# Cross-attention of two layers: the second pair of heads is worked before the sample in every attention step

## The reference, cut to what matters

```
def cross_attend(xn, k, v, wq, wo):
    bsz, L, _ = xn.shape
    q = (xn @ wq).reshape(bsz, L, X_HEADS, X_DH)
    s = jnp.einsum('blhd,bmhd->bhlm', q, k).astype(jnp.float32) * (X_DH ** -0.5)
    p = jax.nn.softmax(s, axis=-1).astype(v.dtype)
    o = jnp.einsum('bhlm,bmhd->blhd', p, v).reshape(bsz, L, D_MODEL)
    return o @ wo
```

## Time and profile before

| | |
|---|---|
| median of 3 runs | 2462.33 us (2460.72 to 2467.35) |
| the profiled execution's own time | 2461.94 us |
| its span in the trace | 2460.2 us |
| TensorE busy | 2294.2 us (93%) |
| VectorE, ScalarE, GpSimd busy | 1215.8, 339.8 and 1220.9 us |
| chain that ended last, TensorE's part | 79% |
| TensorE's mean granted clock | 0.948 of full |

### The profile page before, as it was taken

One profiled execution on the slowest core, in us unless ns is written; L12 is line 12 of the kernel. 1 busy time (PEld: TensorE's weight loads), 2 busy tenths in 40 slices (PEclk: granted clock), 3 DMA queues, 4 the chain that ended last, 5 costly groups with the idle time before them and its releaser, 6 DMA issues.

```text
span 2460.2 us, 39360 instructions
## 1 busy us (share of the span) xinstructions
PE 2294.2 (93%) x16133; PEld 2123.2 (86%) x16133; DVE 1215.8 (49%) x2104; ACT 339.8 (14%) x578; POOL 1220.9 (50%) x1185
## 2 busy tenths in 40 slices
PE   7968768999999999999999989999989999999997
PEld 7967667997999999999999965687569799999996
DVE  6675576432535263674756425441543327253363
ACT  4211301212200000120110131110212210000001
POOL 5535676642665566666656500022025256655562
PEclk8988889999999999999999977889889999999998
DMA  5212323310222222233333321332131012222221
GB/s 189 85 69 86 103 99 121 138 69 35 70 86 86 86 76 78 85 118 141 130 144 148 113 104 52 131 131 86 56 137 69 35 69 73 83 86 86 84 71 54
DMA packets 36594, 231.27 MB, mean 94 GB/s; under 512 B 4332, under 2 KB 7404, under 8 KB 10864
## 3 DMA queue, kind: packets, MB, share of 16 engines
q1 hardware_dynamic: 21600, 154.15, 17.8%
q10 hardware_dynamic: 14864, 75.21, 7.8%
HBM read 195.50 MB, written 33.85 MB: 93 GB/s over the span
## 4 chain that ended last, share of the span: by engine, by line
PE 79%; DVE 16%; issue 2%; ACT 2%; DMA 0%; ACTq 0%; DVEq 0%
PE psum L513 60%; PE psum L543 14%; PE psum L529 2%; DVE hl L1899 1%; DVE xnl L1425 1%; DVE hh L1895 1%; DVE xc L1964 1%; PE psum L539 1%; DVE tm L1625 1%; DVE ss L1410 0%; DVE hr L1888 0%; DVE hs L1891 0%; DVE bbq L1649 0%; DVE tm L2178 0%; DVE tm L2177 0%
## 5 line engine op out<-in xcount | busy, mean ns | idle before, releaser
L463 POOL TENSOR_SCALAR whi<-raw 128x512 fp32r<-128x512 f32 x584 | 422.7, 724 | 1150.1 <-PE psum L513 1107.2
L465 POOL TENSOR_TENSOR wlo<-raw,whi 128x512 fp32r<-128x512 f32 x584 | 803.0, 1375 | 48.7
L513 PE MATMUL psum<-xnh,whi 128*128 128x288 f32 (+1 forms) x2816 | 625.5, 300 | 64.2 <-DVE xnl L1425 17.8
L513 PE MATMUL psum<-xnl,whi 128*128 128x288 f32 (+1 forms) x2816 | 618.7, 298 | 0.0
L513 PE MATMUL psum<-xnh,wlo 128*128 128x288 f32 (+1 forms) x2816 | 618.2, 298 | 0.0
L513 PEld LDWEIGHTS psum<-xnh,whi 128*128 128x128 f32 x2816 | 465.5, 192 | 74.2 <-issue 52.2
L513 PEld LDWEIGHTS psum<-xnl,whi 128*128 128x128 f32 x2816 | 464.9, 192 | 0.0
L513 PEld LDWEIGHTS psum<-xnh,wlo 128*128 128x128 f32 x2816 | 464.4, 191 | 0.0
L513 PE MATMUL psum<-hh,whi 128*128 128x288 f32 x1024 | 220.2, 296 | 1.6 <-DVE hl L1899 1.6
L513 PE MATMUL psum<-hl,whi 128*128 128x288 f32 x1024 | 219.3, 295 | 0.0
L513 PE MATMUL psum<-hh,wlo 128*128 128x288 f32 x1024 | 219.3, 295 | 0.0
(11 more groups left out here) (395 smaller groups left out, 2735.0 us busy)
## 6 DMA issues: line engine op xcount, KB each, us to landing
raw<-in_w SPq DMA_DIRECT2D x146, 1024.0 KB, 4.7
C<-in_C ACTq DMA_DIRECT2D x4, 1024.0 KB, 4.8
o_cp<-mvt ACTq DMA_DIRECT2D x4, 1024.0 KB, 3.9
o_cs<-C ACTq DMA_DIRECT2D x4, 1024.0 KB, 3.9
t_xc<-xc ACTq DMA_DIRECT2D x3, 1152.0 KB, 6.5
t_z<-mv ACTq DMA_DIRECT2D x3, 1152.0 KB, 4.1
t_q<-mq ACTq DMA_DIRECT2D x3, 1152.0 KB, 4.1
t_k<-mk ACTq DMA_DIRECT2D x3, 1152.0 KB, 4.2
```

The source lines that it names most:

```text
L463: pool.tensor_scalar(whi[:, s, c], raw[:, s, c], 1.0, 1.0, ALU.mult, ALU.mult).then_inc(S("slab_hi"), 1)
L465: ins = pool.tensor_tensor(wlo[:, s, c], raw[:, s, c], whi[:, s, c].bitcast(F32), ALU.subtract)
L513: ins = pe.matmul(bank(g, 2 * m + b)[:, 0:t1 - t0], W[wi][:, kk, m0 + m, :], r[:, kk, t0:t1], start=(at_first and wi == 0 and r is rh), st ...
```

## The change

The order of the parts becomes first pair, second pair, sample (0, 1, 2) in every step, on every engine and in the order of groups. Nothing is added or removed. The wait of the first output projection asks for all three parts from its first tile on.

```diff
-ATT_ORDER = (0, 2, 1)
+ATT_ORDER = (0, 1, 2)
...
-        for x in ("pT", 0), ("score", 2), ("score", 1), ("pv", 0), ("pT", 2), ("pT", 1), ("pv", 2), ("pv", 1):
+        for x in ("pT", 0), ("score", 1), ("score", 2), ("pv", 0), ("pT", 1), ("pT", 2), ("pv", 1), ("pv", 2):
             g("att", l, *x)
...
                 transposed(l, 0)
+                scores(l, 1)
                 g = GR["att", l, "score", 2]
...
-                scores(l, 1)
                 values(l, 0)
+                transposed(l, 1)
                 transposed(l, 2)
-                transposed(l, 1)
+                values(l, 1)
                 values(l, 2)
-                values(l, 1)
                 for i in range(4):
                     project(GR["xo", l, i], SL["xo", l, i], xnh, xnl,
-                            wait=None if i else lambda kk: pe.wait_ge(S("att_o"), 3 * l + (2 if kk < 4 else 3)))
+                            wait=None if i else lambda kk: pe.wait_ge(S("att_o"), 3 * l + 3))
...
                 exps(0)
                 copy_pT(0)
+                exps(1)
                 exps(2)
-                exps(1)
                 high_o(0)
+                copy_pT(1)
                 copy_pT(2)
-                copy_pT(1)
+                high_o(1)
                 high_o(2)
-                high_o(1)
...
+                row_max(1)
                 row_max(2)
-                row_max(1)
+                prob(1)
                 prob(2)
-                prob(1)
                 low_o(0)
+                low_o(1)
                 low_o(2)
-                low_o(1)
```

## The result

The changed kernel took 2478.09 us (median of 18 runs, 2471.85 to 2481.13) against 2466.55 us of the kernel before (median of 18 runs). The ratio is 1.0043, with a 95% interval of 1.0035 to 1.0052: 0.43% slower, 10.6 us (the two medians by themselves lie 11.5 us apart). The time lies in the range, and the slowdown on the forecast side of the 0.3%. The profiled execution took 2477.77 us, with a span of 2476.0 us.

What follows compares the result with a forecast made beforehand. TensorE, with 79% of the chain, was taken to bound the kernel. Stalls of +3.9 us and low clock of +7.0 us gave +10.9 us on the profiled 2461.94, or 2472.8, given as 2473 us; range 2465.5 to 2480.

Steps and rivals of the forecast that it cites:

- The walk through the stalls: TensorE in each layer's attention, from scores to output projection: three stalls replace one hole; +3.9 us with no low clock.
- the transposes of part 1: Second pair's transposes on TensorE: run right behind the values of part 0, no hole, 1.91 us at full clock.
- The third stall: Ahead of the first output projection, which waits for `low_o(1)` and `low_o(2)`: 1.9 us per layer, released by VectorE.
- the second stall: Ahead of the sample's transposes, which inherit the old wait for `low_o(0)`: 2.9 us per layer.
- the sum without any low clock: Both layers, clock always at the upper level: +1.5 us in layer 0, +2.4 in layer 1, +3.9 us in all.
- The clock: TensorE behind the new stalls in both layers: 4.5 low-clock stretches at 1.55 us, +7.0 us.
- the first stall: Ahead of the values of part 0, whose banks `exps(1)` must free: about 3.2 us per layer, released by ScalarE.
- The sum: Whole kernel: +3.9 us of stalls and +7.0 us of low clock, +10.9 us, giving 2473 us.
- Fewer low stretches: Rival, chance 0.24: three stalls per layer come but the clock mostly stays up; +3.9 to +7 us, 2466 to 2469.
- the bank is not the wait: Rival, chance 0.05: `exps(1)` does not hold back the values of part 0; -2.7 us, about 2459 before the clock.
- No effect: Rival, no chance of its own given: saving from transposes moved into the old hole equals the two new stalls.
- More low stretches: Rival, chance 0.11: all six stalls meet a low clock, some twice as long; +14 to +19 us, 2476 to 2481.

Runs made afterwards that it cites:

- doubled exponentials: Changed kernel with the 8 exponentials of the second pair run twice, first into a dead buffer; ratio to the kernel before 1.0097 (1.0084 to 1.0110).
- two halves: Kernel before with the new order only in scores to divisions, ratio 1.0024; or only in transposes, values and splits, ratio 1.0020.
- filled changed kernel: Changed kernel plus 3 unused 512-column matmuls ahead of part 0's values and 2 ahead of the output projection, per layer; ratio to the kernel before 1.0020.
- filled kernel before: Kernel before plus 5 unused 512-column matmuls per layer in its hole ahead of the second pair's transposes; ratio 0.9979 (0.9965 to 0.9993).

## Why the prediction was right

*The walk through the stalls.* The mechanism was right. Every wait that it named came, with its releaser: 3.16 us for 3.2 ahead of the values of part 0, 3.08 for 2.9 ahead of the sample's transposes, the transposes of part 1 without a stall at 1.91 us. The doubled exponentials and the two halves show the causes. The third stall was 2.33 us for 1.9: `low_o(2)` begins 0.25 us behind the end of `low_o(1)`, and the release behind it took 0.3 us for 0.2. The prediction's wording for the second stall does not add up: 4.49 less 1.9 plus 0.7 is 3.3 and not 2.9. The difference is that `low_o(0)` began 2.41 us behind `high_o(0)` before (569.00 - 566.59), held up by `prob(1)`, and 2.10 in the walk and in the changed kernel. The filled changed kernel in layer 0 gives the sum without any low clock: 52.52 us a layer, 105.0 us, against 100.1 us of before with its own low stretches, +4.9 us where the prediction had +3.9.

*The clock.* Predicted were 4.5 stretches at 1.55 us, +7.0 us. The changed kernel's profile has 58.21 + 56.53 - 105.0 = 9.7 us of it, in five stretches. The odds and the price were both off. Over all profiles of this study the first stall (3.16 or 3.17 us) met a low clock in 5 of 8 cases (predicted 0.8), the second (3.08 us) in 11 of 12 (0.8), the third (2.33 us) in 6 of 6 (0.65). The price of the third was mis-sized the most: I took 1.55 us for all, and behind the third it was 2.4 us. From the end of that stall to the end of the first output projection the changed kernel took 15.41 us in layer 0 (608.97 - 593.56) and 15.48 in layer 1, the filled one, at full clock, 13.06 in both. The price of the others came near: 8.80 - 7.11 = 1.7 us.

*The sum.* In the profiles the attentions grew by 14.6 us: 9.1 us of stalls (105.0 against 2 x 47.97 = 95.9 of the filled kernel before) and 5.5 us of clock (9.7 against 4.2). So of the loss five eighths are waits and three eighths the clock that they cost. That the prediction's 10.9 met the measured 10.6 us of the ratio so closely is in part luck. Its terms came out 1.0 us low for the stalls and 2.7 us low for the clock, 3.7 us of the 14.6 that the attentions grew by in the profiles; the ratio does not show these 3.7 us, with a profiled execution of before that lay 4.6 us under its median. Which of its stretches differ from the median run is open, for each run with a trace is a single one.

*The page on the clock.* The Trainium skill (TensorE: Matmul & The Clock Gate, section "HAM oscillation — how this bites in real kernels") describes a kernel whose TensorE waits some 3 to 5 us behind bursts of about 2 us, and starts each burst at the low clock, "Every single K-tile." The traces here show the same in kind behind shorter waits, and not each time: in the changed kernel's profile five of six stalls of 2.33 to 3.16 us met the low clock, and over the study the first one did in 5 of 8 cases.

*The rivals.* "Fewer low stretches" falls with the profile and the ratio (its 7 us lie under the interval's 8.6). That the bank is not the wait falls with the stalls released by ScalarE and with the doubled exponentials. "No effect" falls with the stalls. "More low stretches" (+14 to +19 us) is not what the ratio says, but the one profiled pair, 14.6 us apart in the attention, touches its lower end.

## What to carry to other kernels

Where buffers alternate in a fixed order, the order of production also decides which reader each later write waits for. Write down for every group which one it inherits its banks from before reordering: a short consumer (the sample's four exponentials) between two long ones is a cushion, and moving it to the end took it away at the front and put its tail on the path at the end. Count a stall of TensorE as its length plus the low clock behind it, and look at what comes next: the large matmuls behind a stall lost 1.7 us here, the sample's small ones 3.4 us and the large ones behind them another 1.1 (8.16 against 7.08 us), the output projection's, whose stall stood behind small ones, 2.4 us.

## What the runs showed that I had not expected

Idle TensorE time can be worth filling with work that is thrown away: five extra matmuls of 512 columns per layer made the kernel before 0.21% faster (0.9979, 0.9965 to 0.9993), though the medians differ by only 0.11%. At the low clock the sample's values, 16 matmuls of 64 columns, took 7.09 us against 3.68 us, nearly twice, though TensorE was shown as busy in both cases, and the low stretch around them lasted 10.2 us where behind large ones it lasted 3.4 (the first stall of the changed kernel, 1.7 us lost at half the clock). A matmul of 512 columns on plain 32-bit data takes 0.88 us and leaves two records; a count of records is not a count of instructions.

The odds of the first stall were not those of a coin. It met the low clock in all four profiles in layer 0 and in one of four in layer 1, and in each of the 8 cases it did so where the first scores of that layer, some 45 us earlier, had run at full clock (7.14 us), and did not where these had run partly at the low one (8.83 us). The changed kernel's two, from its timeline of PE:

```profile
516.23 7.14 PE L543 MATMUL psum<-KT,xq 128*128 128x256 f32 x32 [1.84 <-issue]
...
1909.32 8.83 PE L543 MATMUL psum<-KT,xq 128*128 128x256 f32 x32 [1.84 <-issue]
```

So a count such as 5 of 8 is no chance per stall that another kernel could take over. Why the one goes with the other no run tests.
